# Gate and up products of the second feed-forward in pairs of tiles by seven block products

## The reference

```python
def swiglu(h, w_gate, w_up, w_down):
    return (jax.nn.silu(h @ w_gate) * (h @ w_up)) @ w_down

def ffn_sublayer(t, shift, scale, gate, norm_g, w_gate, w_up, w_down):
    h = modulate(rms_norm(t, norm_g), shift, scale)
    return t + gate * (MACARON_WEIGHT * swiglu(h, w_gate, w_up, w_down))
```

## Time and profile before

| | us |
|---|---|
| runs | 1463.57, 1460.26, 1462.38 (median 1462.38) |
| span of the profiled execution, first to last instruction | 1459.6 |
| TensorE busy in it | 1429.1 (98%) |
| VectorE busy | 705.8 (48%) |
| GpSimd busy | 664.1 (46%) |
| ScalarE busy | 265.9 (18%) |
| one full segment of the second feed-forward, period | 65.90 |

### The profile page before, as it was taken

How to read it: one execution, slowest core, us unless ns; L and a number is a source line. 1 busy time by engine, 2 the same in 40 slices (tenths; PEclk the granted TensorE clock), 3 DMA queues, 4 the chain that set the end, 5 groups by cost and what they waited for, 6 DMA issues and landing times.

```text
span 1459.6 us, 19101 instructions
## 1 busy us (share of the span) xinstructions
PE 1429.1 (98%) x7912; PEld 1250.1 (86%) x7912; DVE 705.8 (48%) x1032; ACT 265.9 (18%) x440; POOL 664.1 (46%) x389
## 2 busy tenths in 40 slices
PE   7999999999999999999999999999999999999997
PEld 3699999999999999987898888888898888888886
DVE  2774467467454554246636449625775112112114
ACT  3320010010010010023634321124131000000104
POOL 1363443433433433433610456624738557566661
PEclk9999999999999999999999999999999999999999
DMA  9532353353343343114310278384646323233321
GB/s 350 159 109 63 117 147 117 104 146 104 117 129 121 117 122 116 44 38 125 88 30 1 59 193 224 103 258 155 204 134 187 101 87 101 87 101 101 95 65 58
DMA packets 232563, 174.31 MB, mean 119 GB/s; under 512 B 28664, under 2 KB 212124, under 8 KB 232476
## 3 DMA queue, kind: packets, MB, share of 16 engines
q1 hardware_dynamic: 213296, 142.50, 33.4%
q10 hardware_dynamic: 19180, 30.58, 6.5%
HBM read 155.26 MB, written 17.79 MB: 119 GB/s over the span
## 4 chain that ended last, share of the span: by engine, by line
PE 93%; DVE 3%; ACT 1%; issue 1%; DMA 1%; POOL 0%; SPq 0%; DVEq 0%; POOLq 0%; ACTq 0%
PE ps L888 59%; PE ps L1143 15%; PE ps L1146 4%; PE ps L897 2%; PE ps L920 2%; PE ps L1240 2%; PE ps L1095 1%; PE ps L985 1%; PE ps L976 1%; PE ps L1393 1%; PE ps L1050 1%; PE ps L1347 1%; PE ps L1351 1%; PE ps L1162 1%; DMA x_in<-in_ctx_dram 1%
## 5 line engine op out<-in xcount | busy, mean ns | idle before, releaser
L818 POOL TENSOR_SCALAR w_hi<-w_raw 128x1024 fp32r<-128x1024 f32 (+1 forms) x187 | 211.6, 1131 | 745.2 <-issue 458.4
L821 POOL TENSOR_TENSOR w_lo<-w_raw,w_hi 128x1024 fp32r<-128x1024 f32 (+1 forms) x187 | 451.1, 2413 | 15.6
L888 PE MATMUL ps<-h_hi,w_lo 128*128 128x384 f32 (+1 forms) x1224 | 381.4, 360 | 0.0
L888 PE MATMUL ps<-h_hi,w_hi 128*128 128x384 f32 (+1 forms) x1224 | 378.6, 358 | 0.0
L888 PE MATMUL ps<-h_lo,w_hi 128*128 128x384 f32 (+1 forms) x1224 | 378.4, 358 | 0.0
L888 PEld LDWEIGHTS ps<-h_hi,w_lo 128*128 128x128 f32 x1224 | 221.9, 189 | 23.7 <-issue 2.5
L888 PEld LDWEIGHTS ps<-h_hi,w_hi 128*128 128x128 f32 x1224 | 223.9, 189 | 20.4
L888 PEld LDWEIGHTS ps<-h_lo,w_hi 128*128 128x128 f32 x1224 | 223.7, 189 | 20.4
L2196 DVE SCALAR_TENSOR_TENSOR ps<-ps,silu 128x768 f32<-128x768 f32 (+1 forms) x44 | 36.5, 831 | 254.6 <-PE ps L888 248.4
L2226 DVE SCALAR_TENSOR_TENSOR x<-ps,mod,x 128x512 f32<-128x512 f32 x88 | 64.8, 750 | 168.8 <-PE ps L1146 91.4
L1143 PE MATMUL ps<-act_hi,w_lo 128*128 128x512 f32 x336 | 133.7, 398 | 1.8 <-DVEq L2201 1.8
(11 more groups left out here) (374 smaller groups left out, 1868.4 us busy)
## 6 DMA issues: line engine op xcount, KB each, us to landing
w_raw<-in_ffn_w_gate_dram SPq DMA_DIRECT2D x44, 512.0 KB, 3.9
w_raw<-in_ffn_w_up_dram SPq DMA_DIRECT2D x44, 512.0 KB, 3.9
w_raw<-in_ffn_w_down_dram SPq DMA_DIRECT2D x40, 512.0 KB, 3.6
ada_w<-in_ada_w_dram ACTq DMA_DIRECT2D x32, 512.0 KB, 4.3
w_raw<-in_w_in_dram SPq DMA_DIRECT2D x32, 512.0 KB, 4.1
ada_w<-in_ada_w_dram SPq DMA_DIRECT2D x30, 512.0 KB, 4.8
c_scr<-cp ACTq DMA_DIRECT2D x16, 288.0 KB, 4.1
b_scr<-bt_sb ACTq DMA_DIRECT2D x16, 256.0 KB, 3.9
```

What stands on the lines that cost most here:

```text
L818: pool.tensor_scalar(w_hi[:, s, 0:cols], w_raw[:, s, 0:cols], 1.0, 1.0, ALU.mult, ALU.mult)\
L821: pool.tensor_tensor(w_lo[:, s, 0:cols], w_raw[:, s, 0:cols], w_hi[:, s, 0:cols].bitcast(F32), ALU.subtract).then_inc(w_split, 1)
L888: last = pe.matmul(mv[2], st, mv[part], start=(first and q == 0), stop=(n == len(terms) - 1 and q == 2))
```

## The change

Segment 0 of the second feed-forward keeps its matmuls. The other 18 tiles of gate and up are computed in 18 groups: two gate tiles or two up tiles together, as a 2 x 2 block product (halves of the contraction, 4 slices each, by halves of the tokens, 256 each) by Strassen's identity in Winograd's form, with seven products instead of eight. A product is 4 slices by 3 parts, 12 matmuls of 128x256. The groups alternate gate and up; a full segment has four groups, the last segment two, and then the down projection as before.

What the identity adds: four sums of quarters of `h`, made once, on VectorE in segment 0 (`tiles_of_h`), with their high parts on ScalarE (`tile_hi`); four sums of weight blocks for each group, on VectorE (`weight_sums`, 128x512 each); and the sums of the products behind them, some by accumulating on in the same PSUM bank after ScalarE took a copy (`take_part`), some on VectorE. The high parts of the weight blocks (128x512) move from GpSimd to ScalarE (`hi_block`); GpSimd makes the low parts. The eight half slots of `w_hi` and `w_lo` are a ring. The down projection's weights are split by GpSimd as before. Two semaphores go, one of them with its `sem_inc` ahead of every unit in GpSimd's feed-forward program; some others are merged. The core of the diff:

```diff
 PARTS1, FFN1_JOBS = _parts([(1, SEG, False, False), (NSEG - 1, SEG, True, False), (1, TAIL, False, True)])
-PARTS2, FFN2_JOBS = _parts([(NSEG, SEG, False, False), (1, TAIL, False, False)])
...
+PRODUCTS = ("p1", "p7", "p6", "p4", "p5", "p2", "p3")
+NPROD = len(PRODUCTS)
+SUM_BLOCK = {"p7": 0, "p5": 1, "p6": 2, "p3": 3}
...
+        def block_free(eng, b):
+            if b < 2 * SLOTS:
+                is_done(eng, st_jobs(1) - KD + 2 * (b // 2) + 1)
+                return
+            kind, n, i = BLOCK[b - 2 * SLOTS]
+            if kind == "group":
+                product_done(eng, n, i)
+            else:
+                is_done(eng, st_jobs(n) + 2 * i + 1)
...
+            made = st_units(1)
+            for s in ST_SEGS:
+                tiles = st_tiles(s)
+                for q in st_groups(s):
+                    for i in range(NPROD):
+                        b = group_block(q, i)
+                        pool.wait_ge(block_hi, NPROD * q + i + 1)
...
+                for v in range(4):
+                    r, cols = half_slot(b), tiles * 256
+                    raw_here(pool, n)
+                    block_free(pool, b + tiles // 2 - 1)
+                    pool.tensor_scalar(w_hi[:, r // 2, c], w_raw[:, n % 4, 0:cols], 1.0, 1.0, ALU.mult, ALU.mult).then_inc(hi_made, 1)
...
+            def block_product(q, i, bank, opens, closes):
+                b = group_block(q, i)
+                pe.wait_ge(block_ok, NPROD * q + i + 1)
+                wh, wl = (half_of(w, b).rearrange("p (k c) -> p k c", c=P) for w in (w_hi, w_lo))
+                mh, ml = moving[PRODUCTS[i]]
+                for k in range(HK):
+                    for r, (st, mv) in enumerate(((wl, mh), (wh, ml), (wh, mh))):
+                        last = pe.matmul(st_bank(q, bank), st[:, k, :], mv[:, k, :], start=(opens and k == 0 and r == 0),
+                                         stop=(closes and k == HK - 1 and r == 2), skip_group_check=True)
...
+            def group(q, first):
+                quarters_read(q)
+                block_product(q, 0, "a", True, False)
+                if q == 0:
+                    pe.wait_ge(t_ok, 4)
+                block_product(q, 1, "b", True, False)
+                pe.wait_ge(part_ok, 3 * q + 1)
+                block_product(q, 2, "a", False, False)
+                pe.wait_ge(part_ok, 3 * q + 2)
+                block_product(q, 3, "b", False, True)
+                pe.wait_ge(part_ok, 3 * q + 3)
+                block_product(q, 4, "a", False, False)
+                if first:
+                    j = st_jobs(group_seg(q)) - 1
+                    was_read(pe, j - (j - q % 2) % 4)
+                block_product(q, 5, "c", True, True)
+                pe.wait_ge(quarter_ok, 3 * q + 2)
+                block_product(q, 6, "a", False, True)
...
+                            pe.wait_ge(silu_ok, 2 * (st_groups(s)[-1] + 1))
+                        if j % 4 == 1 and e < 4:
+                            pe.wait_ge(gated_lo, 2 * (st_groups(s)[-1] + 1) - 1)
+                    wh, wl = (half_of(w, st_block(s, v) + k // 2).rearrange("p (k c) -> p k c", c=256) for w in (w_hi, w_lo))
+                    c = slice(P * (e % 2), P * (e % 2) + P)
...
+                for k in range(tiles):
+                    if k % 2 == 0:
+                        pe.wait_ge(gated_lo, 4 * (st_groups(s)[0] // 2 + k // 2 + 1))
+                    for e in range(4):
+                        step(e, k)
...
+            def tile_hi(t):
+                act.wait_ge(t_made, t + 1)
+                i = T_ORDER[t]
+                act.activation(t_hi(i), t_32(i), ACT.Copy).then_inc(t_hi_ok, 1)
...
+            def hi_block(b):
+                if b >= ST_BLOCKS:
+                    return
+                kind, q, i = BLOCK[b]
+                if kind != "group":
+                    return
+                block_free(act, b)
+                if PRODUCTS[i] in RAW_BLOCK:
+                    raw_here(act, group_unit(q) + RAW_BLOCK[PRODUCTS[i]][0])
+                else:
+                    act.wait_ge(sum_ok, 4 * q + SUM_BLOCK[PRODUCTS[i]] + 1)
+                act.activation(half_of(w_hi, b), block_source(q, i), ACT.Copy).then_inc(block_hi, 1)
+            def take_part(q, i, n, bank):
+                product_done(act, q, i)
+                if n == 0 and q >= 2:
+                    act.wait_ge(quarter_ok, 3 * q - 3)
+                act.activation(part_sb[:, q % 2, n, :], st_bank(q, bank), ACT.Copy).then_inc(part_ok, 1)
...
+                def quarter(n):
+                    t, h, src = quarters[n]
+                    c = slice(HT * h, HT * h + HT)
+                    if q % 2 == 0:
+                        if n < 3:
+                            act.wait_ge(quarter_ok, 3 * q + n + 1)
+                        else:
+                            product_done(act, q, 6)
+                        act.activation(silu[:, t, c], src, ACT.Silu).then_inc(silu_ok, 1)
+                    else:
+                        act.wait_ge(gated_ok, 4 * m + n + 1)
+                        act.activation(act_hi[:, f + t, c], src, ACT.Copy).then_inc(gated_hi, 1)
+                b = group_block(q, 0) + 2 * SLOTS
+                take_part(q, 0, 0, "a")
+                hi_block(b)
+                take_part(q, 1, 1, "b")
+                hi_block(b + 1)
+                take_part(q, 2, 2, "a")
+                hi_block(b + 2)
+                hi_block(b + 3)
+                if q % 2 == 0 and m:
+                    act.wait_ge(gated_ok, 4 * m)
+                hi_block(b + 4)
+                quarter(0)
+                hi_block(b + 5)
+                quarter(1)
+                quarter(2)
...
+            def tile_add(i, x0, x1, op):
+                ins = TT(t_32(i), x0, x1, op)
+                t_own[0] += 1
+                ins.then_inc(t_step, 1)
+                dve.wait_ge(t_step, t_own[0])
...
+            def tiles_of_h(f_):
+                b11, b12, b21, b22 = h_block(0, 0), h_block(0, 1), h_block(1, 0), h_block(1, 1)
+                def low(t):
+                    i = T_ORDER[t]
+                    dve.wait_ge(t_hi_ok, t + 1)
+                    TT(t_lo(i), t_32(i), t_hi(i).bitcast(F32), ALU.subtract).then_inc(t_ok, 1)
+                if f_ == 0:
+                    tile_add(0, b12[0], b11[0], ALU.subtract)
+                    tile_add(0, t_32(0), b12[1], ALU.add)
+                    tile_add(0, t_32(0), b11[1], ALU.subtract)
+                    dve.sem_inc(t_made, 1)
+                elif f_ == 1:
+                    tile_add(1, b22[0], t_32(0), ALU.subtract)
+                    tile_add(1, t_32(1), b22[1], ALU.add)
+                    dve.sem_inc(t_made, 1)
+                    tile_add(3, b21[0], t_32(1), ALU.subtract)
+                    tile_add(3, t_32(3), b21[1], ALU.add)
+                    dve.sem_inc(t_made, 1)
+                elif f_ == 2:
+                    tile_add(2, b22[0], b12[0], ALU.subtract)
+                    tile_add(2, t_32(2), b22[1], ALU.add)
+                    tile_add(2, t_32(2), b12[1], ALU.subtract)
+                    dve.sem_inc(t_made, 1)
+                    low(0)
+                else:
+                    for t in range(1, 4):
+                        low(t)
+            def weight_sums(q):
+                if q >= 2:
+                    dve.wait_ge(block_ok, NPROD * (q - 1))
+                a11, a12, a21, a22 = (raw_block(q, f, k) for f in range(2) for k in range(2))
+                s3, s1, s2, s4 = (wsum[:, q % 2, n, :] for n in range(4))
+                for f in range(2):
+                    raw_here(dve, group_unit(q) + f)
+                TT(s3, a11, a21, ALU.subtract).then_inc(sum_ok, 1)
+                TT(s1, a21, a22, ALU.add).then_inc(sum_ok, 1)
+                dve.wait_ge(sum_ok, 4 * q + 2)
+                TT(s2, s1, a11, ALU.subtract).then_inc(sum_ok, 1)
+                dve.wait_ge(sum_ok, 4 * q + 3)
+                TT(s4, a12, s2, ALU.subtract).then_inc(sum_ok, 1)
...
+                if q + 1 in st_groups(group_seg(q)):
+                    weight_sums(q + 1)
+                bank_a, bank_b, bank_c = (st_bank(q, n) for n in "abc")
+                s1, s7, s2, c22 = (part_sb[:, q % 2, n, :] for n in range(4))
+                quarters = ((1, 0, bank_b), (1, 1, c22), (0, 0, bank_c), (0, 1, bank_a))
...
+                def gated(n):
+                    t, h, val = quarters[n]
+                    if n < 3:
+                        dve.wait_ge(quarter_ok, 3 * q + n + 1)
+                    else:
+                        product_done(dve, q, 6)
+                    STT(val, val, 0.5, silu[:, t, HT * h:HT * h + HT], ALU.mult, ALU.mult).then_inc(gated_ok, 1)
+                def low(n):
+                    t, h, val = quarters[n]
+                    c = slice(HT * h, HT * h + HT)
+                    dve.wait_ge(gated_hi, 4 * m + n + 1)
+                    TT(act_lo[:, f + t, c], val, act_hi[:, f + t, c].bitcast(F32), ALU.subtract).then_inc(gated_lo, 1)
```

(53 more changed lines are left out.)

177 lines of the change are left out of this document (167 added, 10 removed).

## The result

The changed kernel takes 1485.6 us, the median of four runs (1484.4 to 1489.4), against 1462.4 for the kernel before: 23.2 us more, a ratio of 1.016 with a 95% interval of 1.0141 to 1.0178. That is slower, and 4.6 us above the 1481 forecast.

What follows compares the result with a forecast made beforehand. TensorE, busy 98% of the span, was taken as the bound. Segment 0 +14.0, TensorE's saving -14.4, full segments +16.0 and last segment +3.0 gave +18.6 us on 1462.4: 1481 us, range 1449 to 1490.

Steps and rivals of the forecast that it cites:

- rival A: Whole kernel: VectorE and GpSimd get past each other, waits fall in gaps, TensorE's gain stands; -11.0, 1451 us; chance 0.26.
- B: Only segment 0 is late and the groups hide their sums; -1.4, 1461 us; chance 0.12.
- signs that the prediction named: Weight sums averaging 1.2 us or more, GpSimd's low parts above 1.29, product 5 waiting 1.5 to 2.5, period 66 to 67.5.
- TensorE's saving: Gate and up groups: 84 matmuls at 0.120 us, 10.08 a group against 10.88; 18 groups save 14.4 us.
- C: Starting a dependent product costs something, such as 0.1 us at each of 126; 1464 or 1494 us; chance 0.07.
- D: The 256-column matmul goes at half the price in this stretch, 10 us less, 1471 us; chance 0.04.
- Segment 0: Sums of h in VectorE's queue delay conditioning adds and the fourth down job; 4.4 to 16.0 us longer, 14 taken.
- the walk: Step-by-step timing of segment 0 and the groups, VectorE and GpSimd taking turns; segment 0 16.0 us longer, full segments 4.9.
- First group: First group of a segment: third sum late, so product 5 starts at 7.65 us instead of 5.76; 1.9 us lost.
- Third group: Third group of a segment: held-up sums make the second and third copies late; 1.4 to 2.4 us lost.
- Seam: Fourth group to down jobs: GpSimd's down units hold up VectorE, so low parts come late; up to 1.7 us lost.
- Last segment: First group loses 1.9 us, and the down projection's start lies bare 1.9 to 2.4; 1.4 to 3.8, 3.0 taken.

Runs made afterwards that it cites:

- c22_psum: The changed kernel with the fourth quarter of a pair read from its PSUM bank instead of from a copy in SBUF: 1479.0 us, ratio 1.0106 to the kernel before.
- copy_first: The changed kernel with ScalarE's copies of a pair's first two quarters ahead of the high parts that wait for sums: 1469.0 us, ratio 1.0029.
- no_sums: The changed kernel without the four sums of weight blocks of each pair, raw blocks in their place: 1470.9 us, ratio 1.0055 to the kernel before.
- tiles_only: The kernel before plus only segment 0's sums, low and high parts of h, results unused: 1482.0 us, ratio 1.0119.
- one_input: The kernel before plus the fourteen VectorE operations on h, each with one SBUF input instead of two, results unused: 1475.3 us, ratio 1.0091.

## Why the prediction was right, and where it was off

*Direction and cause.* Slower by the hold-up of VectorE and GpSimd, as forecast; rival A (1451) and B (1461) are out. Most signs that the prediction named came: weight sums at means of 1.22 to 1.52 us, GpSimd's 512 column low parts at 1.41 and 1.53, the wait ahead of product 5 released by ScalarE's copy (at 1.34 and 0.96 us less than the 1.5 to 2.5 named), a period of 67.0. c22_psum shows the mechanism at the seam, copy_first and no_sums at product 5; tiles_only shows which operations cost segment 0 its time.

*TensorE's saving.* 10.08 us a group forecast. A full segment's four groups take 43.15 us with 2.6 of stalls, so 10.14 each: near enough right. Rivals C and D are out with it, as products start without a gap where their inputs are there.

*Segment 0.* +14 taken, 16.0 by the walk; +15.0 to the fourth down job. The conditioning sums began at 1133.2 on the clock of before (1137.01 less 3.9) where the walk had 1136, the fourth down job at 1145.1 where it had 1146. That the end fits so well is in part luck, as two steps of the walk miss and offset each other. The four additions behind feature tile 1 were to take turns with GpSimd and last 9.0 us; they took 5.1, as GpSimd stood for the late down unit (on the clock of before it came near 1126, not 1123). Against that adds 6 and 7 took 3.8 instead of 2.4, and the three additions and the low part behind them 9.8 instead of 8.0. What the sum lacked is a term for the half clock behind the stalls, 2.1 us: segment 0 cost 17.1 where 14 was taken.

*First group.* The walk has product 5 at 7.65 us, 1.9 lost; it started 7.25 behind the group's first matmul, 1.5 lost. Third group: 1.4 to 2.4 forecast, 1.1 measured. Seam: up to 1.7 forecast, 1.96 measured. Together 4.6 less the 0.6 that went, 4.0 a segment as taken. The measured four segments are still 2.8 us above the forecast's +3.2 (16.0 less 16 groups' saving of 12.8): 1.0 of it in the groups' pitch, and some 1.6 in one segment whose seam wait was followed by half clock.

*Last segment.* Forecast +1.4 (3.0 less two groups' saving of 1.6), measured +1.2, with the 1.5 at product 5 and a wait of 1.43 at its first down job.

*The sum.* The three lines of the table came to 24.3 us where the terms made 18.6: 3.1 more in segment 0, 2.8 in the full segments, 0.2 less in the last one. 3.7 of these 5.7 us are half clock, for which the prediction had no term. Its offset of 2.8 us from the span to the time isn't fixed either: the changed kernel's profiled execution stands 1.7 above its own span.

*What it did not ask.* The prediction's rule is that two inputs in SBUF are held up and that one in PSUM frees the operation; both held. What lies between, one input that is in SBUF, it left open, and the expectation of one_input had that wrong. Nothing of the sum hung on it, since all the added operations had two. And rival A's period of a full segment (62 to 63 us) can be reached for a reason that A did not have: "VectorE and GpSimd get past each other" is false, yet with ScalarE's copies put first the groups lose little (62.94), near to what the prediction named as its sign of being wrong, that "no copy is late".

*Still open.* That copy_first frees the seam by the moment at which the fourth quarter's operations meet GpSimd's units is read from the trace; shifting them alone wasn't tried. How much of segment 0's loss is hold-up and how much the operations' own time is estimated only. And whether segment 0 can hold the sums of h without a wait at all: four orders behind the conditioning adds were tried.

## What to carry to other kernels

A product saved on TensorE is paid in additions elsewhere; count these beside what GpSimd does in the same stretch, and with each held up by up to a whole operation of the other engine (here 512 columns from 0.69 to 1.79 us, 1024 from 1.22 to 3.4) unless an operand lies in PSUM. Slow operations cost nothing by themselves: of the 23 us, 19 came back by letting one engine do what is ready before what must wait for them. And put operations that are needed later behind the ones on which TensorE waits now, but look at the next wait before counting the gain.

## What the runs showed of the hardware

- TensorE's clock was granted at half, 1.2 GHz, behind stands of 7.1, 4.9 and, once in four times, 1.8 us in the changed kernel, and behind stands of 2.7 (three kernels), 4.4 and 6.1 us in the others. The matmuls' pitch was then 0.427 us instead of 0.2267, for 5 to 10 of them in a row; behind the stands of 4.9 and 1.8 us it cost 2.1 and 1.6 us on top. The stalls of 1.3 us ahead of product 5 had none behind them.
- A product of 1024 columns of one SBUF input with a column of constants took 0.76 us, an addition of two such inputs 1.22; beside GpSimd they took up to 2.8 and 3.4. With an input in PSUM, 256 columns kept 0.41 to 0.43 us beside GpSimd, where the SBUF form of the low part took up to 2.61.
- 256-column matmuls of this kind, a new weight load to each, kept 0.120 us in all five segments.
